# Attention probabilities: scaling and transposing, or one product with a diagonal matrix of reciprocal sums

## The reference

```python
def joint_softmax(*logits):
    m = functools.reduce(jnp.maximum, [s.max(axis=-1, keepdims=True) for s in logits])
    e = [jnp.exp(s - m) for s in logits]
    inv = 1.0 / functools.reduce(jnp.add, [t.sum(axis=-1, keepdims=True) for t in e])
    return [t * inv for t in e]
...
def diff_attend(q, kv_parts, lam):            # layer 0, 4 heads with two maps each
    logits = [jnp.einsum('bqhmd,bkhmd->bmhqk', q, k).astype(F32) * scale for k, _ in kv_parts]
    probs = joint_softmax(*logits)
    outs = [jnp.einsum('bhqk,bkhd->bqhd', (p[:, 0] - lam * p[:, 1]).astype(v.dtype), v)
            for p, (_, v) in zip(probs, kv_parts)]
...
    p_loc, p_ctx, _ = joint_softmax(s_loc, s_ctx, s_sink)   # layer 0, 8 heads, window and sink
...
def mla_attend(qn, qr, kv_parts):             # layer 1, 16 heads, 64 + 32 wide
```

## Time and profile before

| | |
|---|---|
| median of 3 runs | 2531.6 us (2529.41 to 2533.87) |
| profiled execution: its own time / its span | 2527.8 us / 2525.8 us |
| layer 0 attention | about 192 to 345 us of the span |
| layer 1 attention | about 912 to 976 us |
| expert weights stream at about 428 GB/s | from about 1600 us to the end |
| PE, DVE, ACT busy, whole span | 2053.2, 759.7, 443.5 us |
| PE transposes at L772 (all groups) | 272 instructions, 41.2 us busy |

### The profile page before, as it was taken

The page is one execution under the profiler, slowest core; times in us unless marked ns, Lnnn a source line. Parts: engine busy times, 40 slices in busy tenths (PEclk is TensorE's granted clock), DMA queues, the critical chain, the costliest instruction groups (busy, mean ns, idle before and its releaser), DMA issues.

```text
span 2525.8 us, 28670 instructions
## 1 busy us (share of the span) xinstructions
PE 2053.2 (81%) x11775; PEld 1285.2 (51%) x11775; DVE 759.7 (30%) x1667; ACT 443.5 (18%) x959; POOL 7.0 (0%) x15
## 2 busy tenths in 40 slices
PE   6998899999999999899999997865566565555555
PEld 3544368888747857898877776411111111111111
DVE  3217734555302555685036523000000000001001
ACT  3004534001011455211132221100000000000000
POOL 0000000000000000000000000000000000000000
PEclk9999999999999999999999988977787777778787
DMA  9557861332222521444622322899999999999996
GB/s 382 197 200 295 316 223 34 100 100 61 77 85 43 167 84 52 130 132 119 219 100 93 115 100 111 360 428 428 427 429 427 428 428 428 428 428 427 428 427 284
DMA packets 178514, 614.97 MB, mean 243 GB/s; under 512 B 26096, under 2 KB 119536, under 8 KB 144592
## 3 DMA queue, kind: packets, MB, share of 16 engines
q1 hardware_dynamic: 177568, 610.38, 61.9%
q0 software_dynamic: 816, 2.76, 0.4%
HBM read 612.06 MB, written 1.05 MB: 243 GB/s over the span
## 4 chain that ended last, share of the span: by engine, by line
PE 57%; DMA 33%; DVE 7%; ACT 2%; issue 1%; SPq 0%; DVEq 0%; ACTq 0%
PE ps L360 55%; DMA ring<-in_expert_w_up 14%; DMA ring<-in_expert_w_gate 9%; DMA ring<-in_expert_w_down 8%; PE ps L772 1%; DMA ring<-in_ada_w 1%; DVE AR L950 1%; DVE AR L953 1%; DVE AR L952 1%; DVE ring L951 1%; DVE ST L807 0%; DVE AR L718 0%; DVE X L719 0%; ACT AR L825 0%; ACT AR L837 0%
## 5 line engine op out<-in xcount | busy, mean ns | idle before, releaser
L360 PE MATMUL ps<-ring,AR 128*32 128x256 f32 (+2 forms) x4384 | 581.6, 631 | 360.6 <-DMA ring<-in_expert_w_up 133.5
L360 PEld LDWEIGHTS ps<-ring,AR 128*32 128x32 f32 (+1 forms) x4384 | 197.1, 135 | 719.5 <-issue 246.0
L360 PE MATMUL ps<-H,ring 128*128 128x256 f32 (+2 forms) x2240 | 513.5, 388 | 7.6 <-ACT H L656 5.1
L360 PEld LDWEIGHTS ps<-H,ring 128*128 128x128 f32 x2240 | 403.9, 192 | 103.8 <-issue 55.0
L360 PE MATMUL ps<-AR,ring 128*128 128x256 f32 (+2 forms) x1548 | 358.5, 389 | 3.9 <-DVE AR L962 2.9
L360 PEld LDWEIGHTS ps<-AR,ring 128*128 128x128 f32 x1548 | 273.3, 191 | 84.3 <-issue 53.1
L360 PE MATMUL ps<-AR 128*128 128x128 f32 (+5 forms) x1168 | 171.3, 332 | 25.2 <-ACT AR L825 8.6
L2187 DVE TENSOR_TENSOR AR<-AR,ps 128x512 f32<-128x512 f32 x16 | 11.0, 687 | 585.6 <-PE ps L360 585.6
L360 PEld LDWEIGHTS ps<-AR 128*128 128x128 f32 (+2 forms) x1168 | 126.3, 184 | 56.0 <-issue 47.3
L2198 DVE TENSOR_TENSOR AR<-ps,X 32x256 f32<-32x256 f32 x64 | 26.9, 420 | 280.7 <-PE ps L360 279.0
L2173 ACT ACTIVATE AR<-ps 128x512 f32<-128x512 f32 x16 | 9.6, 597 | 528.4 <-PE ps L360 528.4
(11 more groups left out here) (284 smaller groups left out, 1443.9 us busy)
## 6 DMA issues: line engine op xcount, KB each, us to landing
ring<-in_expert_w_gate SPq DMA_DIRECT2D x64, 2048.0 KB, 23.4
ring<-in_expert_w_up SPq DMA_DIRECT2D x64, 2048.0 KB, 23.3
ring<-in_expert_w_down SPq DMA_DIRECT2D x64, 2048.0 KB, 23.2
ring<-in_ada_w SPq DMA_DIRECT2D x36, 2048.0 KB, 10.1
ring<-in_ffn_w SPq DMA_DIRECT2D x44, 1024.0 KB, 7.7
ring<-in_w_in SPq DMA_DIRECT2D x12, 2048.0 KB, 7.9
ring<-in_ffn_w SPq DMA_DIRECT2D x16, 1408.0 KB, 7.1
ring<-in_ab_w_in SPq DMA_DIRECT2D x4, 2048.0 KB, 16.0
```

What stands on the lines that cost most here:

```text
L360: m = nc.tensor.matmul(out_, lhsT=lhsT, rhs=rhs, start=start, stop=stop)
```

## The change

The probabilities in `PR` are no longer scaled. DVE builds in a new tile `DG` (two buffers, two 128x128 matrices) the identity times the reciprocal sums, with a factor of minus lambda in the second matrix of a "b" group. PE turns and scales a block in one ordinary product: the block is the stationary operand and the diagonal matrix the moving one. In a "b" group each output block is the sum of two products, one a map.

```diff
+        DG = sb("DG", [P, 2, 2, P])
...
                 for u in range(len(g.vals)):
                     b = take(pe, ("t", g.key, u))
                     pe.wait_ge(probs_ready.sem, self.prob[i] + u + 1)
+                    maps = (u,) if len(g.vals) == 2 else (0, 1)
                     for j in range(g.nk // P):
-                        m = nc.tensor.transpose(ps[:, b, j * P:(j + 1) * P], PR[:, i % 2, u, j * P:(j + 1) * P], ident)
-                    m.then_inc(bank_full[b], 1)
+                        for m in maps:
+                            mm(ps[:, b, j * P:(j + 1) * P], PR[:, i % 2, m, j * P:(j + 1) * P], DG[:, i % 2, m, :],
+                               m == maps[0], m == maps[-1], b if (j, m) == (g.nk // P - 1, maps[-1]) else None)
...
-                p = [PR[:, i % 2, m, 0:g.nk] for m in range(2)]
+                d = [DG[:, i % 2, m, :] for m in range(2)]
                 if len(g.vals) == 2:
                     for u in range(2):
-                        c.mark(V.tensor_scalar(p[u], p[u], st[:, 4 + u:5 + u], None, ALU.mult), probs_ready, self.prob[i] + u + 1)
+                        c.mark(V.tensor_scalar(d[u], ident, st[:, 4 + u:5 + u], None, ALU.mult), probs_ready, self.prob[i] + u + 1)
                 else:
-                    c.step(V.tensor_tensor(st[:, 5:6], st[:, 5:6], LAM[:, 6:7], ALU.mult))
-                    c.step(V.tensor_scalar(p[0], p[0], st[:, 4:5], None, ALU.mult))
-                    c.mark(V.scalar_tensor_tensor(out=p[0], in0=p[1], scalar=st[:, 5:6], in1=p[0], op0=ALU.mult, op1=ALU.add),
-                           probs_ready, self.prob[i] + 1)
+                    c.step(V.tensor_scalar(d[0], ident, st[:, 4:5], None, ALU.mult))
+                    c.mark(V.tensor_scalar(d[1], ident, st[:, 5:6], LAM[:, 6:7], ALU.mult, ALU.mult), probs_ready,
+                           self.prob[i] + 1)
```

## The result

| | before | after |
|---|---|---|
| median of 4 runs each on one chip | 2531.7 us (2529.4 to 2533.9) | 2562.4 us (2561.1 to 2564.5) |
| profiled execution: own time / span | 2527.8 / 2525.8 us | 2561.35 / 2559.6 us |
| layer 0 attention, first row maximum to last L501 | 192.93 to 344.27: 151.3 us | 192.17 to 364.01: 171.8 us |
| layer 1 attention, first scores to L569 | 912.39 to 975.19: 62.8 us | 932.19 to 1008.26: 76.1 us |
| DVE / PE busy, whole span | 759.7 / 2053.2 us | 740.3 / 2096.7 us |

The ratio is 1.0129, 95% interval 1.0117 to 1.0141. The prediction was 2534.5 us with a range up to 2540; the kernel is 30.7 us slower by the medians. By the spans of the two profiled executions it is 33.8 us, and the two attentions hold all of it: 20.5 + 13.3 = 33.8 us. (The profiled execution of before is one of its quicker ones, 3.9 us under its median.

The account below looks back on a forecast made before the run. PE was taken to bound both attentions, with a few gaps made by DVE. PE's 7.3 us less DVE's 4.2 gave +3.1 us: 2530.9 for the profiled execution, 2534.5 on the median's scale, range 2526.5 to 2540.

Parts of the forecast that it names:

- The step that failed: Turns of both attentions on PE: a plain 128x128 float32 product costs 111.5 ns, from 0.89 us for 8.
- 1.5 to 4 ns more each: The 272 turns where one product replaces one transpose: 0.4 to 1.1 us in all, 0.8 taken.
- The term of PE: Both attentions: PE's bill of 7.3 us, from 6.2 for 48 added products, 0.8 for 272 replaced turns, 0.3 for exposed loads.
- The prediction's own sign of being wrong: In the changed kernel's profile, turns that need over 0.118 us a product would show the forecast wrong.
- The second rival: All 320 turns of both attentions fall to the stationary operand's load, 191 ns a product: 25 us, 2560 us; chance 0.05.
- The fourth rival: Products with the diagonal run at a quarter of the transposes' pace: +110 us less the gains, 2638 us; chance 0.01.
- DVE's new forms: DVE's 128-column instructions that build the diagonal matrices: about 286 ns with one scalar, 347 ns with two.
- the DVE work removed: Scaling work taken off DVE in all groups of both attentions: about 20 us, hardly any of it on the path.
- the pauses at 198, 201, 216, 222 and 263 us: PE's waits for DVE in layer 0 shrink by 0.8, 0.58, 0.25, 0.4 and 1.24 us, in that order.
- the DVE gain as a whole: Both attentions: the part of DVE's saving that reaches the end, 4.2 us, or 3.5 to 5.0 at the bounds.
- The first rival: DVE was the real pacemaker, pacing 7 of the 16 "b" groups in layer 0: -4.6 us, 2527 us; chance 0.17.
- The fall at about 222 us: Layer 0, granted clock 0.66 on average from 222 to 227: 1.5 us less if the shorter pause avoids it, even chance.

Follow-up runs that it names:

- transposes twice: The kernel before, with every one of the 272 transposes issued twice to the same place: 2552.7 us, ratio 1.0083.
- DVE's part alone: Kernel before, but DVE builds the diagonal matrices instead of scaling; PE transposes unscaled probabilities, without the second map of "b" groups: 2524.9 us, ratio 0.9973.
- the bf16 diagonal: The changed kernel with exponentials and diagonal matrices in bfloat16, the sum in PSUM still float32: 2521.7 us, ratio 0.9963.

## Why the prediction was wrong

**The step that failed** is the price in "A plain 128x128 product in a stream costs the distance between starts, 1046.22 - 1045.33 = 0.89 us for 8, or 111.5 ns". The distance is right and the divisor isn't: these 8 rows are 4 products. A product costs 223 ns in a stream, 235 in the turn. Both sides of the comparison were then read in different units, one transpose against half a product, and "1.5 to 4 ns more each" became 114 ns. The term of PE, 7.3 us, should have been 640 x 0.1115 - 272 x 0.109 = 41.7 us, plus what the low clock adds. With that the same sum gives 2527.8 + 41.7 + 1.5 - 4.2 - 1.5 = 2565 us against 2561.4 measured for the profiled execution; of the 4 us left, 1.1 are waits for ACT that shrank in layer 0 (9.8 us before, 8.7 after). The prediction's own sign of being wrong, turns over 0.118 us a product, is what the trace shows: 0.235.

The number could have been caught ahead of the run, with the rows on record. The chain's group of layer 1 has 20 records for two score products and eight value products. And PE's order printed for the changed kernel has x8 at the first turn, for 4 blocks and two maps, where the trace of any float32 product would have had 16; for the scores that order has x2 a group where the timeline has x4. Whoever puts a count from the program beside a count from the trace sees the factor.

**The rivals.** The second rival gave 2560 us, close to the time, by a mechanism that isn't there: PE would fall to the load's 191 ns. The pace in the turn is 118 ns a record with loads of 196 ns, and it is 115 when the loads take 142 ns (transposes twice). The number agreed by luck: 320 x 0.08 + 3 = 29 us and 368 x 0.11 less 6.5 us of waits = 34 us happen to be near each other; had only the time been compared, the wrong mechanism would have passed. The fourth rival, a quarter of the transposes' pace, is refuted in size: in the turn it is 235 against 121 ns, a factor of 1.9. The Trainium skill (TensorE: Matmul & The Clock Gate, Terms) says of the transpose mode that it is four times faster for FP32; the trace has a factor of 2 for 128x128 blocks. Its advice in Perfetto Trace Analysis, section Transposes, to make a logical transpose a transpose and not a standard matmul, agrees with the run that changes only this: +25 us. I argued the rule away with a row that I had misread; a rule that contradicts a row is a reason to count the row again.

**What held.** PE is the bound of both attentions, and a microsecond lost there arrives at the end: 20.5 + 13.3 us by the stages, 33.8 us by the spans. The chain goes over to the loads of the expert weights later by as much, at 1622.44 in place of 1588.68 us, 33.8 us:

```profile
1617.96 4.47 PE ps L360 x37
1622.44 11.56 DMA ring<-in_expert_w_up
```

DVE's new forms, the DVE work removed (19.4 us of the 20 forecast), the pauses at 198, 201, 216, 222 and 263 us and the DVE gain as a whole (4.2 forecast; with DVE's part alone 2.6 by the stages, 4.3 to 9.1 by the ratio, 3.8 in layer 0 by PE's waits) came out as worked out. The first rival, DVE as pacemaker, wanted 8.7 us from DVE and the clock; the ratio of DVE's part alone just reaches that, but its stages and waits have a third to a half of it, and nothing of that size could cover 41 us.

**Open:** the clock. The fall at about 222 us isn't in the execution of the changed kernel, for which the prediction gave an even chance. The columns of these windows are those of the earlier trace rows; after has

```profile
220.00:230.00 10.00, 8.12 (x64) 5.40 (x63) 5.14 (x15) 3.54 (x12) 0.00 (x0) 1.00 0.66 240
```

and the bf16 diagonal, with the same pause of 1.88 us (before the product at 220.64),

```profile
220.00:230.00 10.00, 9.13 (x54) 4.21 (x58) 7.22 (x21) 4.51 (x11) 0.00 (x0) 0.83 0.94 350
```

The granted clock is 1.00 in one and 0.83 in the other. The kernel with only the "b" groups changed has the same PE work as the changed one up to there, and 0.83 from 223 to 233 us where the changed one has 1.00. So the pause's length alone doesn't decide it. It is worth 1.5 us or so in one execution.

The prediction counted with the two falls of one trace. They don't belong to the program alone: the kernel with only the "m" groups changed runs the same program as before in layer 0, with the same waits (24.8 us), and its trace has a granted clock of 0.95 from 275 to 310 us where before has 1.00; the stage takes 153.4 us there in place of 151.3 (193.24 to 346.66). So a stage of layer 0 in a single trace carries some 2 us of clock, and that its sum above closes to 0.8 us is in part luck.

## What to carry to other kernels

Before a duration in the trace is made the price of an operation, put the trace's count of that row beside the number of calls in the program: here a plain float32 product is two matmuls and two loads, a float32 transpose or a bf16 product is one. Moving work off an engine that isn't the bound onto the one that is needs the right price of the new form, because nearly every instruction of it is paid: here 368 records for 33 us. A difference of 2 us in one stage of one trace may be the clock: look at the granted clock of the stretch before giving it a cause. And when a forecast's rival hits the time, look for its mechanism before it is believed.

## What the runs showed of the hardware

- A turn of a 128x128 block on PE, from start to start of the turns in the layer 1 groups, so with the step to the next work: float32 transpose 121 ns, two of them 230 ns (943.45 to 945.29 us for eight), plain float32 product 235 ns, the product cut in two along the columns 453 ns, plain bf16 product 68 ns.
- Inside a stream at a granted clock of 1.00, from record to record: float32 transpose 109 ns, float32 record 112 ns with 128 columns and also 112 ns with 64, 429 ns with 512 columns; bf16 record 56 ns with 128 columns. At a granted clock of 0.50 the 64-column records take 218 ns (198.21 to 205.20 us for 32).
- Products with a stationary operand 64 wide that write two different halves of the partitions start 6 or 7 ns apart and share the 109 ns of one record.
- Float32 to bf16 is a factor of 235 / 68 = 3.5 for a block in a turn, and 2 x 112 / 56 = 4.0 in a stream. At 2.4 GHz the 429 ns of a 512-column float32 record are 2.0 clock periods a column, the 56 ns of a 128-column bf16 record 1.05. The Trainium skill (FP8 and Floating Point Precision, TensorE Precision Notes) says that true FP32 takes four passes through the array. The trace agrees if each of the two records is two passes; it shows the two periods a column, not the passes.
- A DVE `tensor_scalar` from SBUF to SBUF in float32: 287 ns with 128 columns, 353 with 256, 486 with 512; a second scalar from memory adds 59 ns; with bf16 in and out 353 ns at 512 columns.
